# Gathered token rows on every second partition, and the last rows loaded by broadcast

## The reference, cut to what matters

```python
sh1, sc1, g1, sh2, sc2, g2 = split(silu(cond) @ w_ada + b_ada, 6)      # one set for context, one for latent tokens
x = x + g1 * attention(modulate(x, n1, sh1, sc1))
h = modulate(x, n2, sh2, sc2)
gates = top2_of_the_best_group(sigmoid(h @ w_router) + b_router)        # (tokens, 16), two nonzero each
hid = silu(einsum('nd,edf->nef', h, w_gate)) * einsum('nd,edf->nef', h, w_up)   # 1024 -> 512
x = x + g2 * einsum('nef,efd->nd', hid * gates[..., None], w_down)      # 512 -> 1024
# after both layers:
y = x * rsqrt(mean(x * x) + eps) * final_norm_g
```

## Time and profile before

| what | value |
|---|---|
| median of 3 runs | 1019.36 us (1019.11 to 1020.76) |
| the profiled execution, its own time | 1020.74 us |
| its span in the profile | 1018.9 us |
| busy: PE, DVE, ACT, POOL | 946.5, 346.1, 253.1, 131.9 us |
| HBM read and written | 300.01 MB, 17.26 MB |
| expert part of layer 0, and of layer 1 | about 270 to 520 us, and 775 to 1019 us |

### The profile page before, as it was taken

One profiled execution on the slowest core, in us unless ns is written; L12 is line 12 of the kernel. 1 busy time (PEld: TensorE's weight loads), 2 busy tenths in 40 slices (PEclk: granted clock), 3 DMA queues, 4 the chain that ended last, 5 costly groups with the idle time before them and its releaser, 6 DMA issues.

```text
span 1018.9 us, 13500 instructions
## 1 busy us (share of the span) xinstructions
PE 946.5 (93%) x5209; PEld 462.1 (45%) x5209; DVE 346.1 (34%) x862; ACT 253.1 (25%) x604; POOL 131.9 (13%) x151
## 2 busy tenths in 40 slices
PE   4899989999999999988779998999999999999895
PEld 3345535555533334333354554555554343433342
DVE  2231077531662122212152004755138222121227
ACT  2220055431411111111151103554132111111124
POOL 4131000001211111101024100000121111111101
PEclk9799999999999999999999999999999999999999
DMA  9960377688899999999985025867947999999994
GB/s 352 394 232 21 137 273 275 220 337 351 325 383 389 394 392 400 396 413 413 381 309 204 21 83 188 310 224 263 419 189 270 371 390 387 411 399 408 415 405 168
DMA packets 58568, 313.64 MB, mean 308 GB/s; under 512 B 6826, under 2 KB 9094, under 8 KB 27520
## 3 DMA queue, kind: packets, MB, share of 16 engines
q1 hardware_dynamic: 50208, 288.54, 72.7%
q0 software_dynamic: 7424, 21.01, 5.8%
q10 hardware_dynamic: 864, 3.15, 0.8%
HBM read 300.01 MB, written 17.26 MB: 311 GB/s over the span
## 4 chain that ended last, share of the span: by engine, by line
PE 74%; DMA 17%; DVE 3%; issue 2%; ACT 1%; SPq 1%; POOL 1%; ACTq 0%; POOLq 0%; DVEq 0%
PE psum L1145 15%; DMA arena<-in_w_up 9%; PE psum L1570 8%; PE psum L1211 8%; PE psum L1423 8%; PE psum L1395 4%; PE psum L1386 4%; PE psum L1058 3%; PE psum L1541 3%; PE psum L1506 3%; DMA arena<-in_w_ada 3%; PE psum L1518 3%; PE psum L1157 2%; DMA arena<-token_rows,row_i 2%; PE psum L1085 1%
## 5 line engine op out<-in xcount | busy, mean ns | idle before, releaser
L1145 PE MATMUL psum<-arena 128*64 128x512 f32 x480 | 220.3, 609 | 10.5 <-DMA arena<-in_w_up 10.4
L1148 PE MATMUL psum<-arena 128*64 128x512 f32 x480 | 220.5, 609 | 0.0
L1145 PEld LDWEIGHTS psum<-arena 128*64 128x64 f32 x480 | 65.6, 140 | 153.5 <-issue 150.5
L1211 PE MATMUL psum<-arena 128*64 128x512 f32 x480 | 110.9, 600 | 2.0 <-ACT arena L1740 0.9
L2209 DVE SCALAR_TENSOR_TENSOR arena<-arena,psum 64x512 f32<-64x512 f32 (+2 forms) x32 | 22.9, 714 | 240.6 <-ACT arena L1734 240.6
L1570 PE MATMUL psum<-arena 128*128 128x384 f32 x256 | 84.0, 488 | 0.6 <-PE psum L1570 0.6
L1423 PE MATMUL psum<-arena 128*128 128x384 f32 x256 | 83.4, 487 | 0.6 <-PE psum L1423 0.6
L1734 ACT ACTIVATE arena<-psum 64x512 f32<-64x512 f32 (+2 forms) x32 | 19.8, 618 | 246.2 <-PE psum L1148 224.6
L1148 PEld LDWEIGHTS psum<-arena 128*64 128x64 f32 x480 | 65.6, 140 | 0.0
L1423 PEld LDWEIGHTS psum<-arena 128*128 128x128 f32 x256 | 48.3, 190 | 34.6 <-issue 1.8
L1570 PEld LDWEIGHTS psum<-arena 128*128 128x128 f32 x256 | 48.2, 190 | 34.9 <-issue 2.5
(11 more groups left out here) (323 smaller groups left out, 1180.9 us busy)
## 6 DMA issues: line engine op xcount, KB each, us to landing
arena<-in_w_down SPq DMA_DIRECT2D x64, 1024.0 KB, 28.9
arena<-in_w_gate SPq DMA_DIRECT2D x64, 1024.0 KB, 26.6
arena<-in_w_up SPq DMA_DIRECT2D x64, 1024.0 KB, 27.5
arena<-in_w_ada SPq DMA_DIRECT2D x24, 2048.0 KB, 8.2
arena<-in_w_in SPq DMA_DIRECT2D x6, 2048.0 KB, 16.1
arena<-in_w_out SPq DMA_DIRECT2D x4, 2048.0 KB, 8.2
arena<-expert_rows SPq DMA_DIRECT2D x12, 512.0 KB, 11.1
arena<-in_w_in SPq DMA_DIRECT2D x2, 1664.0 KB, 14.0
```

What stands on the lines that cost most here:

```text
L1145: ins = nc.tensor.matmul(bank[b][0:MAIN, :], hg[:, k, 0:MAIN], row(wg[half], k), start=(k == 0), stop=(k == KD - 1))
L1148: ins = nc.tensor.matmul(bank[b][MAIN:P, :], hg[:, k, 0:MAIN], row(wu[half], k), start=(k == 0), stop=(k == KD - 1))
L1211: ins = nc.tensor.matmul(bank[6][MAIN * j:MAIN * j + MAIN, :], hidT[:, c, 0:MAIN], down_row(w[half], c)[:, 512 * j:512 * j + 512], start=( ...
```

## The change

**Gathers.** A gather of 64 slots writes partitions 0, 2, ..., 126, and one of 32 slots partitions 0, 4, ..., 124. Gathers of 96 slots stay as they are. The transposes take all partitions up to 128 (twice the width for most units), and the copies to `hg` pick every second column (or fourth) of PSUM. Scatters stay as they are.

**The rows of the end.** The diagonals, the six products and the six copies go. ACT stores `g2` without its bias to a new HBM tensor `gates` (two stores of 4 KB, right behind `copy_rows`), and `router_weights` waits until they have landed. SP, behind its last weight load and before it waits for the last scatter, waits for places 13 and 14 and for that store, and issues four loads that read one row of 4 KB for all 128 partitions (512 KB written each): the bias, the two gates and the gain. DVE adds the bias to both gates (`gate_biases`) behind the gating of unit 15 and before `y_copy(14)`; for this it waits for all four loads. `x_early` now waits only until unit 14 has been gated.

```diff
+        def row_step(u):
+            return 1 if slots_of(u) == CAP else P // slots_of(u)
+
+        def turned(b, u):
+            return tiles(b, 4)[:, :, 0:row_step(u) * slots_of(u):row_step(u)]
...
+            def end_rows():
+
+                sp.wait_ge(slot_free, max(loads.last(DEPTH - 1, p) for p in END_ROW_PLACES) + 1)
+                sp.wait_ge(gates_stored, 32)
+                sp.dma_start(bias_row, a["b_ada"][DEPTH - 1, 5 * D:6 * D].partition_broadcast(P)).then_inc(end_rows_in, 16)
+                for s in (1, 0):
+                    sp.dma_start(gate_row[s], gates.ap()[s, :].partition_broadcast(P)).then_inc(end_rows_in, 16)
+                sp.dma_start(gain_row, a["final_norm_g"].partition_broadcast(P)).then_inc(end_rows_in, 16)
...
+            end_rows()
             for i in range(2):
                 sp.wait_ge(y_out[i], 16 * (E_ALL - SUMMED) // 2 * DEPTH)
...
-                    pool.indirect_dma_start(x_of(u)[0:slots_of(u), :], None, h_rows.ap(),
+                    pool.indirect_dma_start(x_of(u)[0:row_step(u) * slots_of(u):row_step(u), :], None, h_rows.ap(),
...
-                n = slots_of(q % UNITS_E)
+                n = row_step(q % UNITS_E) * slots_of(q % UNITS_E)
                 x = x_of(q % UNITS_E)[0:n, :].rearrange("t (p k) -> t k p", k=KD)
                 for k in range(KD):
-                    ins = nc.tensor.transpose(bank[4 + k // 4][:, CAP * (k % 4):CAP * (k % 4) + n], x[:, k, :], ident[0:n, 0:n])
+                    ins = nc.tensor.transpose(bank[4 + k // 4][:, P * (k % 4):P * (k % 4) + n], x[:, k, :], ident[0:n, 0:n])
...
-            def gate_rows():
-
-                pe.wait_ge(hid_ready, unit_of(DEPTH - 1, LAST[0]) + 1)
-                for n in range(6):
-                    s, half = divmod(n, 2)
-                    pe.wait_ge(diag_ready, s + 1)
-                    if n >= 3:
-                        pe.wait_ge(row_ready, n - 2)
-                    nc.tensor.matmul(bank[ROW_BANK[n]], ones, end_row[s][:, 512 * half:512 * half + 512],
-                                     start=True, stop=True).then_inc(row_ps, 1)
...
             def x_early():
 
-                pe.wait_ge(row_ready, 6)
+                pe.wait_ge(hid_ready, unit_of(DEPTH - 1, LAST[0]) + 1)
...
                 nc.scalar.activation(ada_rows, bank[7], ACT.Copy).then_inc(ada_rows_ready, 1)
+                if (l, r) == (DEPTH - 1, ADA_ROUNDS - 1):
+                    act.wait_ge(ada_rows_ready, ADA_ROUNDS * DEPTH)
+                    for half in range(2):
+                        at = COND_COLS * (2 + half)
+                        act.dma_start(gates.ap()[:, 512 * half:512 * half + 512], ada_rows[at:at + 2, :]).then_inc(gates_stored, 16)
...
-                    if ends and u == LAST[0]:
-                        for n in range(6):
-                            s, half = divmod(n, 2)
-                            act.wait_ge(row_ps, n + 1)
-                            nc.scalar.activation(end_row[s][:, 512 * half:512 * half + 512], bank[ROW_BANK[n]], ACT.Copy).then_inc(row_ready, 1)
...
+                if l == DEPTH - 1:
+                    dve.wait_ge(gates_stored, 32)
                 v.tensor_tensor(w_rg, w, gain[:, 1, :, :].unsqueeze(3).to_broadcast(each), ALU.mult).then_inc(w_rg_ready, 1)
...
-                v.tensor_copy(hg[:, 4:8, 0:n], bank[5][:, 0:4 * CAP].rearrange("p (k n) -> p k n", k=4)[:, :, 0:n]).then_inc(hg_dve, 1)
+                v.tensor_copy(hg[:, 4:8, 0:n], turned(bank[5], q % UNITS_E)).then_inc(hg_dve, 1)
...
-                    if ends and u == LAST[0]:
-                        gate_diagonals()
+                    if ends and u == LAST[1]:
+                        gate_biases()
                     if u == 0:
                         spare_units(l)
                     if i:
                         y_copy(unit_of(l, units[i - 1]))
...
+            def gate_biases():
+
+                dve.wait_ge(end_rows_in, 64)
+                for s in (1, 0):
+                    v.tensor_tensor(gate_row[s], gate_row[s], bias_row, ALU.add).then_inc(gates_ready, 1)
...
-                dve.wait_ge(row_ready, 4)
+                dve.wait_ge(gates_ready, 2)
```

More of the change, by code:

```diff
@@ L42 @@
 OUT_PIECES = 2
-GATE_ROW_PLACE, GAIN_ROW_PLACE = 13, 14
+END_ROW_PLACES = (13, 14)
 END_BANK = (0, 4, 2)
 END_ORDER = (1, 0, 2)
-ROW_BANK = (0, 1, 7, 0, 1, 7)
 LAST_ROWS = MAIN + TAIL
@@ L197, in plan_loads, with build @@
     return t
-def build(nc, a, outs, scratch, h_rows, y_rows):
+def build(nc, a, outs, scratch, h_rows, y_rows, gates):
     f32, i32 = mybir.dt.float32, mybir.dt.int32
@@ L278, in build @@
         end_lo = tiles(ring[:, 6 * SMALL:6 * SMALL + NT * D], NT)
-        end_row = [gate_row[0], gate_row[1], gain_row]
+        bias_row = bias_flat[:, 2 * D:3 * D]
         slot_gate = xg[1]
@@ L396, in build @@
         stored, y_ready = sem("stored"), sem("y_ready")
-        diag_ready, row_ps, row_ready = (sem(n) for n in ("diag_ready", "row_ps", "row_ready"))
+        gates_stored, end_rows_in, gates_ready = (sem(n) for n in ("gates_stored", "end_rows_in", "gates_ready"))
         mix_gated, tile_gated, pair_gated, pair_ps = (sem(n) for n in ("mix_gated", "tile_gated", "pair_gated", "pair_ps"))
@@ L877, in end_gates @@
                     pool.wait_ge(y_mixed, 2 * NT * l + NT * again + 1)
-                    pool.wait_ge(row_ready, 6)
+                    pool.wait_ge(gates_ready, 2)
                     pool.tensor_tensor(end_hi[:, 0, :], end_hi[:, 0, :], gate_row[0], ALU.mult).then_inc(mix_gated, 1)
@@ L1313, in experts @@
                             settle(units[i - 1])
-                    if ends and u == LAST[0]:
-                        gate_rows()
                 if units[-1] == LAST[1] and l + 1 < DEPTH:
@@ L1717, in copy_slots @@
                 if u < FIRST_UNITS:
-                    n, b = slots_of(u), 4 if u else 6
+                    n = slots_of(u)
                     for c, done in ((0, hg_act), (4, hg_dve)):
-                        nc.scalar.activation(hg[:, c:c + 4, 0:n], bank[b + c // 4][:, 0:4 * CAP].rearrange("p (k n) -> p k n", k=4)[:, :, 0:n],
-                                             ACT.Copy).then_inc(done, 1)
+                        rows_T = turned(bank[4 + c // 4], u) if u else tiles(bank[6 + c // 4][:, 0:4 * CAP], 4)[:, :, 0:n]
+                        nc.scalar.activation(hg[:, c:c + 4, 0:n], rows_T, ACT.Copy).then_inc(done, 1)
                     return
                 n = slots_of(q % UNITS_E)
-                nc.scalar.activation(hg[:, 0:4, 0:n], bank[4][:, 0:4 * CAP].rearrange("p (k n) -> p k n", k=4)[:, :, 0:n],
-                                     ACT.Copy).then_inc(hg_act, 1)
+                nc.scalar.activation(hg[:, 0:4, 0:n], turned(bank[4], q % UNITS_E), ACT.Copy).then_inc(hg_act, 1)
             def gate_tanh(q):
@@ L1756, in y_copy, with experts @@
                 ins.then_inc(y_act, 1)
-            def experts(l, units, ends=False):
+            def experts(l, units):
                 copy_slots(unit_of(l, units[0]))
@@ L1866, in _ @@
                     copy_rows(l + 1, 0)
-                experts(l, list(range(AHEAD)), ends=l == DEPTH - 1)
+                experts(l, list(range(AHEAD)))
                 if l == DEPTH - 1:
@@ L2245, in experts @@
                 y_copy(unit_of(l, units[-1]))
-            def gate_diagonals():
-                dve.wait_ge(slot_free, loads.last(DEPTH - 1, GATE_ROW_PLACE) + 1)
-                each = [P, KD, P]
-                final_gain = vec[:, 2, 16:16 + KD]
-                for s, by_feature in enumerate((mod[:, 5, :, 0], mod[:, 5, :, 1], final_gain)):
-                    if s == 2:
-                        dve.wait_ge(slot_free, loads.last(DEPTH - 1, GAIN_ROW_PLACE) + 1)
-                    v.tensor_tensor(tiles(end_row[s], KD), ident.unsqueeze(1).to_broadcast(each), by_feature.unsqueeze(2).to_broadcast(each),
-                                    ALU.mult).then_inc(diag_ready, 1)
+            def gate_biases():
+                dve.wait_ge(end_rows_in, 64)
+                for s in (1, 0):
+                    v.tensor_tensor(gate_row[s], gate_row[s], bias_row, ALU.add).then_inc(gates_ready, 1)
             def slot_gates():
@@ L2296, in end_norm @@
             def end_norm(again):
-                dve.wait_ge(row_ready, 6)
                 for i, t in enumerate(END_ORDER):
@@ L2556 @@
     y_rows = nc.dram_tensor("expert_rows", (2 * TOK, D), f32, kind="Internal")
-    build(nc, args, outs, scratch, h_rows, y_rows)
+    gates = nc.dram_tensor("gate_values", (2, D), f32, kind="Internal")
+    build(nc, args, outs, scratch, h_rows, y_rows, gates)
     r = run(nc, [arrays], core_ids=[0])
```

## The result

The kernel after took 1014.15 us (median, 1011.73 to 1015.94 in five runs), the kernel before 1019.58 us beside it (1019.11 to 1020.76). The ratio is 0.9943, 95% interval 0.9926 to 0.9960: it became 5.4 us faster by the medians (4.1 to 7.5 by the interval), where I had forecast 1031.1 us in a range from 1017 to 1037. The profiled execution took 1011.73 us, with a span of 1009.9.

The account below looks back on a forecast made before the run. Weight transfers bound the expert parts, a chain through DVE the end. +0.6 (ACT) +9.2 (broadcasts, additions) +1.9 (clock) +0 (gathers) = +11.7 us on 1020.74, 1032.4, less 1.4 for the median: 1031.1 us, range 1017 to 1037.

Parts of the forecast that it names:

- Which end is nearer?: Gathers in the expert parts: chose 0 gain from the moved slots, out of 0 to about 8.3 us per layer.
- my bound: Most the changed gathers could gain, adding up their slow windows: 8.4 us in layer 0, 8.2 in layer 1.
- my first paragraph: Expert parts: a shorter DMA stream gains in full while below PE's waits for weights, about 10 and 5 us.
- The rival's 16.6: Gathers of both layers: gain if their dips vanish, 8.3 us per layer, set against 11.7 lost.
- Rows behind the last weights: End: four broadcast loads queue behind the weights, land by 1001.3; additions end at 1003.8, `y_copy(14)` 9.2 us late.
- with 2.5 us each: End, rival of slow broadcasts: 2.5 us per load instead of 1.24, +5.0 us, 1036 us; chance 0.13.
- Clock at 0.50: End, PE after idling: slow clock adds 1.5 us on unit 15's `down`, 0.4 on transposes ahead, 1.9 in all.
- My sum for this half: The end with ACT's store: +0.6 for ACT, +9.2 for broadcasts and additions, +1.9 for the clock, +11.7 us.
- by 994.6 at the latest: End, PE: `down(14)` finishes by 994.6, then PE has nothing to do until 1004.5.
- ACT's store: Store of the gates: two issues on ACT delay PE, +0.6 us; landing some 1.4 us late for DVE, costed 0.
- The gathers' dips vanish: Rival for the expert parts' gathers: spreading slots removes 8.3 us per layer, 1014.5 us in all; chance 0.20.
- Its own sign: Evidence given for the rival of vanishing dips: all DMA engines are busy in the dips yet move less.

Follow-up runs that it names:

- experiments 1: Kernel before with only the spread gathers, wider transposes and their copies, the end as it was: 1006.85 us, ratio 0.9872.
- 3: Four kernels, the kernel before with gathers side by side on other partitions (middle, upper half, a place per unit, all centred): 1005.3, 1022.9, 1018.0, 1005.18 us.
- (4): Two kernels, `padded` and `probe_two`, the kernel before with absent indices added to gathers, in the second also other places: 1011.67 and 1015.26 us.
- experiment 2: Kernel after with its gathers on side-by-side partitions from 0 again, so the end's change alone: 1029.83 us, ratio 1.0098 against the kernel before.
- experiment 6: Kernel after with the two bias additions moved behind `y_copy(14)` on DVE: 1013.39 us, ratio 0.9939 against the kernel before.
- `padded`: Kernel before, filled rows and their partitions unchanged, each gather given 128 slots by absent indices: 1011.67 us in one run.
- `probe_two`: Kernel before with gathers placed or padded differently unit by unit; unit 7's 64 slots on 32 to 95 plus 32 absent on 96 to 127: 1015.26 us, one run.
- `balanced`: Kernel before with every gather centred, side by side: 64 slots from partition 32, 96 from 16, 32 from 48: 1005.18 us, ratio 0.9858.

## Why the prediction was wrong

**The failed step** is the one under "Which end is nearer?": "The dip looks like a price per gathered row and not like one for which partitions are written. I take 0, and keep 8.3 for the range." The dips are no price of the rows. They went with the places of the slots, for the same rows (experiments 1, 3), and even with rows and places unchanged (4). Two readings led me there. I took the 96-slot gather as a row for "reaches further up", but 0 to 95 is twice as dense below as above and dips like 0 to 63. And I read unit 15's smaller dip as in proportion to its rows; it has fewer slots as well, and the gathers of before could not tell the two apart.

In place of the 0 the runs show -13.3 us with the old end (1), and -15.7 us with the new one (from 2 to the kernel after).

**The size of the gathers' gain** was near my bound, 8.4 and 8.2 us of dips. With the old end 13.3 us came of it, by the profile 7.9 ahead of layer 1's first gather (765.0 on before's clock against 772.93) and 5.2 behind. Layer 1 gave less than its 8.2, because PE had waited only 5.1 us for weights there; past that a faster stream gains nothing, as my first paragraph says. With the new end this limit does not hold, since the rows stand behind the stream: 16.7 us by the landing of the last row, 10.1 of it in layer 0 and 6.6 in layer 1. The rival's 16.6 was the right sum for that end.

**The end** was right in its main steps. Rows behind the last weights: landing at 1002.2 against 1001.3, `y_copy(14)` at 1004.4 against 1003.8 (2). The broadcasts cost no more than ordinary loads, as I had taken: with 2.5 us each they would have landed 5 us later. Clock at 0.50, 3.64 us for products of 1.94: 1.7 us where I had 1.5. The transposes ahead of them took 0.47 us against 0.42, so my 0.4 for these was too much; the 1.9 of the forecast is what was lost behind `y_copy(14)` in all. My sum for this half was 11.7. The measurement is 9.7 by the medians, with 2.2 us of uncertainty either way, and 11.7 from table load to the end of the span in the two profiles (769.4 against 757.7). Two things were put wrongly. I wrote of the instructions queued behind the additions, and experiment 6 shows that their order does not matter. And PE did not finish `down(14)` "by 994.6 at the latest": in experiment 2 it ended at 996.7 on before's clock, because it waited for weights in unit 15 and its clock was already 0.50 in `down(14)` (5.42 us for 16 products of 3.65). The rows landed later still and hid it.

**ACT's store** was costed at 0.6 us; its two issues took 0.75. DVE then waited 0.40 us for it, where I had 1.4 us late and hidden.

```profile
692.69 0.75 ACTq L1686 DMA_DIRECT2D gate_values<-arena  x2
...
698.50 0.43 DVE L1962 TENSOR_TENSOR arena<-arena 128x256 f32<-128x256 f32 x1 [0.40 <-DMA gate_values<-arena]
```

**The rival** "The gathers' dips vanish" had it, with 1014.5 us against 1014.15. Its two terms were right within the noise: 16.6 for the gathers against 15.7 to 16.7, 11.7 for the end against 9.7 to 11.7. That it came within 0.4 us is luck, for each term is uncertain by some 2 us, and the layers shared the gathers' gain as 10.1 and 6.6, not by halves. I gave it 0.20. Its own sign (all engines busy and yet moving less) was the better evidence: a stall of engines that a place can cure looks like that, and extra bytes of rows do not, since these count in the GB/s. The rule of the Trainium skill (SBUF — State Buffer, Door 1: The DMA port swizzle) pointed to it too. The trace agrees in part: 0 to 63 and 64 to 127 dip, 32 to 95 and every second partition do not. As a rule on which partitions are written it does not cover `padded`, where the rows stay on the low partitions and the dip goes.

So the change has one half that gains 13 us by itself and one that gives 7 of them back (1014.15 against 1006.85 for the gathers alone). The best kernel that ran is the one with the gathers spread, the 96-slot ones padded, and the end of before, 1004.37 us; that with centred gathers (1005.18) and the gathers alone (1006.85) can't be told from it.

## What to carry to other kernels

Where gathers run beside a stream that sets the pace, try to put their slots evenly over the 128 partitions, and look at the GB/s while they are in flight: at full busy share, a lower rate is not the price of the bytes, and another placement may cure it. If the rows must stay where they are, absent indices up to 128 do it as well, for a few gathers. Before a small computation is replaced by a load, ask which queue it will stand in and who is idle: here 5 us of products on TensorE, which lay wholly or by half in the shadow of weights, were traded for 2 MB on the one resource that was full.

## What the runs showed of the hardware

- A gather with an index for a row that does not exist still has its part in the traffic: the queue of the gathers has 706 more packets in 160 us for the 704 more absent indices of `padded`, and 32 of them on partitions 96 to 127 go with a rate of 328 GB/s over 4 us where it was 422 without them (unit 7 of layer 1, `probe_two` and `balanced`).
- The rate falls for the weights too, which go to all 128 partitions by another queue: a 64-slot gather at 0 to 63 moves about 0.25 MB, and the core moves 0.36 MB less in the 4 us, its rows counted in. The weights' queue moved 1.06 MB in such a window of the kernel before (799.2 to 803.2) and 1.55 MB in one without a gather (867 to 871).
- 32 slots on partitions 32, 34 to 94 dip (378 and 385 GB/s), on 0, 4 to 124 not (421 and 418). No rule that I tried covers both this and the 64 slots on 32 to 95.
- The scatters, which read partitions 0 to slots - 1 in every kernel, do not lower the rate: the kernel after reads 424 GB/s in the window 4 us behind its first scatter's issue in layer 1 (785.25), when no gather is in flight.
